# One 512-column matmul for both operand parts in the last products of the 256-token stages

## What is computed

```
h = h + 0.5 * (silu(n @ w_gate) * (n @ w_up)) @ w_down      # feed-forward, 2816 wide
h = h + concat(y_ret, y_diff) @ w_out                       # mixer of the first block
h = h + (b_gate * conv) @ w_out                             # short convolution
h = h + o @ w_out                                           # dilated attention
```

## Time and profile before

| | us |
|---|---|
| median of 3 runs | 2353.56 (2352.23 to 2355.72) |
| the profiled execution | 2352.63 |
| its span (first to last instruction) | 2350.8 |
| PE busy | 2292.0 (97%) |
| PE weight load busy | 2218.0 (94%) |
| DVE busy | 1527.3 (65%) |
| ACT busy | 1161.2 (49%) |

### The profile page before, as it was taken

The page is one execution under the profiler, slowest core; times in us unless marked ns, Lnnn a source line. Parts: engine busy times, 40 slices in busy tenths (PEclk is TensorE's granted clock), DMA queues, the critical chain, the costliest instruction groups (busy, mean ns, idle before and its releaser), DMA issues.

```text
span 2350.8 us, 42875 instructions
## 1 busy us (share of the span) xinstructions
PE 2292.0 (97%) x18162; PEld 2218.0 (94%) x18162; DVE 1527.3 (65%) x2626; ACT 1161.2 (49%) x1826; POOL 35.3 (2%) x47
## 2 busy tenths in 40 slices
PE   7999999999999998999999999999999899999999
PEld 7999878999999987999999999999999798988999
DVE  6665966665665675766676587656665666665763
ACT  5444455444544454644554445445444556564542
POOL 0000000100000000000000000000000000000000
PEclk9999999999999999999999999999999999999999
DMA  8545423865555432554565465555555444452653
GB/s 279 177 155 172 144 90 113 260 212 176 177 171 170 158 126 73 186 190 163 174 214 173 157 216 196 182 170 191 195 173 158 137 139 138 141 167 81 215 188 99
DMA packets 423454, 393.65 MB, mean 167 GB/s; under 512 B 14015, under 2 KB 419647, under 8 KB 423264
## 3 DMA queue, kind: packets, MB, share of 16 engines
q1 hardware_dynamic: 412240, 375.56, 49.5%
q0 software_dynamic: 11024, 15.36, 2.1%
HBM read 389.66 MB, written 7.41 MB: 169 GB/s over the span
## 4 chain that ended last, share of the span: by engine, by line
PE 91%; DVE 6%; ACT 2%; issue 1%; DMA 1%; SPq 0%; DVEq 0%; ACTq 0%
PE ps L1236 28%; PE ps L1237 28%; PE ps L1238 28%; DVE t L805 2%; PE ps L1480 1%; PE ps L1500 1%; PE ps L1455 1%; PE ps L1491 0%; PE ps L1482 0%; PE ps L1502 0%; PE ps L1347 0%; PE ps L1348 0%; PE ps L1340 0%; DVE t L833 0%; DMA t<-ffn_w_gate 0%
## 5 line engine op out<-in xcount | busy, mean ns | idle before, releaser
L1236 PE MATMUL ps<-t 128*128 128x256 f32 (+1 forms) x5696 | 1638.6, 288 | 21.8 <-DVE t L805 17.1
L1237 PE MATMUL ps<-t 128*128 128x256 f32 (+1 forms) x5696 | 1626.0, 285 | 0.0
L1238 PE MATMUL ps<-t 128*128 128x256 f32 (+1 forms) x5696 | 1621.0, 285 | 0.0
L1236 PEld LDWEIGHTS ps<-t 128*128 128x128 f32 x5696 | 1080.4, 190 | 39.1 <-issue 29.7
L1237 PEld LDWEIGHTS ps<-t 128*128 128x128 f32 x5696 | 1078.7, 189 | 5.2 <-issue 4.4
L1238 PEld LDWEIGHTS ps<-t 128*128 128x128 f32 x5696 | 1079.3, 189 | 0.0
L805 DVE TENSOR_TENSOR t<-t 128x1024 fp32r<-128x1024 f32 (+1 forms) x728 | 862.1, 1196 | 184.7 <-ACT t L550 183.1
L550 ACT ACTIVATE t<-t 128x1024 fp32r<-128x1024 f32 (+1 forms) x728 | 737.7, 1029 | 315.3 <-PE ps L1238 303.8
L625 ACT ACTIVATE t<-t 128x256 fp32r<-128x256 f32 (+1 forms) x176 | 74.5, 423 | 307.2 <-DVE t L931 307.2
L928 DVE TENSOR_TENSOR t<-ps,t 128x256 f32<-128x256 f32 (+1 forms) x176 | 75.6, 430 | 128.3 <-PE ps L1238 128.3
L921 DVE TENSOR_TENSOR t<-ps,t 128x256 f32<-128x256 f32 (+1 forms) x176 | 75.7, 430 | 116.0 <-PE ps L1238 114.9
(11 more groups left out here) (155 smaller groups left out, 978.2 us busy)
## 6 DMA issues: line engine op xcount, KB each, us to landing
t<-ffn_w_in SPq DMA_DIRECT2D x88, 1024.0 KB, 5.2
t<-ffn_w_gate SPq DMA_DIRECT2D x43, 1024.0 KB, 5.2
t<-ffn_w_up SPq DMA_DIRECT2D x43, 1024.0 KB, 5.4
t<-attn_w_qkv SPq DMA_DIRECT2D x72, 512.0 KB, 3.6
t<-ffn_w_down SPq DMA_DIRECT2D x32, 1024.0 KB, 5.3
t<-ffn_w_out SPq DMA_DIRECT2D x32, 1024.0 KB, 5.3
t<-w_in SPq DMA_DIRECT2D x28, 1024.0 KB, 4.9
t<-ffn_w_down SPq DMA_DIRECT2D x16, 768.0 KB, 4.8
```

The source lines that it names most:

```text
L1236: pe.matmul(o, hi, xhi, start=i == 0, stop=False)
L1237: pe.matmul(o, hi, xlo, start=False, stop=False)
L1238: ins = pe.matmul(o, lo, xhi, start=False, stop=i == r.nk - 1)
```

## The change

In the last products of the stages with 256 tokens (feed-forward stages 5, 6, 8, 9 and 11, mixer stage 4, convolution stage 7, dilated stage 10) a group has two matmuls in place of three. The first multiplies the high weight part with both operand parts, 512 columns in one instruction, over the whole bank: columns 0 to 255 get hi.xhi, columns 256 to 511 hi.xlo. The second adds lo.xhi to columns 0 to 255. DVE adds each half of the bank to `h` with an instruction of its own; the second waits for the first, and it, not the first, counts up `evac`. All other products stay as they were.

```diff
-                        dve.scalar_tensor_tensor(h[:, m, c0:T], ps[:, r.banks[j], 0:T - c0], scale, h[:, m, c0:T],
+                        ins = dve.scalar_tensor_tensor(h[:, m, c0:T], ps[:, r.banks[j], 0:T - c0], scale, h[:, m, c0:T],
+                                                       ALU.mult, ALU.add)
+                        if c0 == 0:
+                            ins.then_inc(S["evac"], 1)
+                        else:
+                            ins.then_inc(S["dve"], 1)
+                            own.up()
+                    for j in range(r.n if c0 else 0):
+                        m = r.first - first + j
+                        w.wait_ge(S["dve"], own.n - r.n + 1 + j)
+                        dve.scalar_tensor_tensor(h[:, m, c0:T], ps[:, r.banks[j], SEQ:2 * SEQ], scale, h[:, m, c0:T],
                                                  ALU.mult, ALU.add).then_inc(S["evac"], 1)
...
-                        pe.matmul(o, hi, xhi, start=i == 0, stop=False)
-                        pe.matmul(o, hi, xlo, start=False, stop=False)
+                        if both is None:
+                            pe.matmul(o, hi, xhi, start=i == 0, stop=False)
+                            pe.matmul(o, hi, xlo, start=False, stop=False)
+                        else:
+
+                            pe.matmul(ps[:, r.banks[j], :], hi, both(k), start=i == 0, stop=False)
                         ins = pe.matmul(o, lo, xhi, start=False, stop=i == r.nk - 1)
...
-                        matmuls(r, range(FCH), lambda k: (a[:, k, 0, 0:N], a[:, k, 1, 0:N]), ready)
+                        matmuls(r, range(FCH), lambda k: (a[:, k, 0, 0:N], a[:, k, 1, 0:N]), ready,
+                                both=(lambda k: a[:, k, :, 0:N]) if N == SEQ else None)
...
+                            (lambda k: y[:, k, :, cq:T]) if NQ == SEQ else None)
...
+                            both=lambda k: c_yy[:, k, :, :])
...
+                            both=lambda k: d_y[:, k, :, :])
```

More of the change, by code:

```diff
@@ L1218, in _, with matmuls @@
             w = Waits(pe)
-            def matmuls(r, order, operand, ready, hook=None):
+            def matmuls(r, order, operand, ready, hook=None, both=None):
                 N = T - r.c0
@@ L1426, in mixer @@
                         w.wait_ge(S["hn"], at(l, "r", 3))
-                    matmuls(r, OUT_ORDER, lambda k: (y[:, k, 0, cq:T], y[:, k, 1, cq:T]), ready, hook if m == 0 else None)
+                    matmuls(r, OUT_ORDER, lambda k: (y[:, k, 0, cq:T], y[:, k, 1, cq:T]), ready, hook if m == 0 else None,
+                            (lambda k: y[:, k, :, cq:T]) if NQ == SEQ else None)
             def conv(s):
@@ L1439, in conv @@
                 for r in runs[21:]:
-                    matmuls(r, range(KC), lambda k: (c_yy[:, k, 0, :], c_yy[:, k, 1, :]), ready)
+                    matmuls(r, range(KC), lambda k: (c_yy[:, k, 0, :], c_yy[:, k, 1, :]), ready,
+                            both=lambda k: c_yy[:, k, :, :])
             def dilated(s):
@@ L1517, in dilated @@
                         w.wait_ge(S["hyl"], NH)
-                    matmuls(r, range(KC), lambda k: (d_y[:, k, 0, :], d_y[:, k, 1, :]), ready)
+                    matmuls(r, range(KC), lambda k: (d_y[:, k, 0, :], d_y[:, k, 1, :]), ready,
+                            both=lambda k: d_y[:, k, :, :])
             w.wait_ge(S["square"], 16)
```

## The result

| | before | after |
|---|---|---|
| median of 19 runs, us | 2353.31 (2351.8 to 2355.72) | 2358.56 (2354.33 to 2361.51) |
| ratio | | 1.0022, 95% interval 1.0015 to 1.0029 |
| span of the profiled execution, us | 2350.8 | 2356.9 |

The kernel became slower by 5.2 us, 0.22%. I had forecast 0.5 us less, had given 0.60 to no measurable change and 0.15 to slower. The time lies inside the range, at its upper end, and just inside the case that had 0.15; the likeliest case was wrong.

What follows compares the result with a forecast made beforehand. PE's matmuls were taken to bound the kernel. -10.4 (fixed part) + 2.3 + 3.9 (DVE) + 0.7 (last evictions) = -3.5 us; 3.0 us of low clock makes -0.5, so 2353.1 us, range 2345 to 2359.5.

Steps and rivals of the forecast that it cites:

- The DVE part: Second evictions delay the low weight part PE waits for: 2.3 us more in stage 4, 3.9 in stages 7 and 10.
- PE's head start: In stages 7 and 10 PE is earlier by 24 groups x 11.8 ns = 0.28 us, taken off DVE's delay.
- the low part of the fourth tile: Low weight part from DVE for the next stage's first run; PE starts on it 2.3 us later in stage 4.
- the last evictions: At the kernel's end four evictions in place of two, 0.33 us apart: 0.7 us more before the last transfer.
- The term that failed is the fixed part of the wide matmul: Time a 512-column matmul holds PE besides its columns: 11.8 ns, saving 10.4 us over 880 feed-forward groups.
- My bounds: Limits of the 512-column matmul's fixed part from plain float32 rows: 3.3 ns saves 17.9 us, 20 ns saves 3.3 us.
- The slower rival: Fixed part 20 ns, a group saves 3.7 ns, and the waits come: +7.0 us, 2360.6 us; chance 0.13.
- The clock's sum: PE's new waits bring two low-clock stretches, behind stage 4 and one of stages 7 and 10: 3.0 us more.
- A wide matmul without a fixed part: Rival: the 512-column matmul has nearly no fixed part (3.3 ns), -8.4 us, 2345.2 us; chance 0.15.
- delays that don't reach PE: Rival: slack in the ACT and DVE chain hides DVE's delays, -9.7 us, 2343.9 us; chance 0.07.
- no low clock: Rival: PE's new waits bring no stretch at 1.2 GHz, -3.5 us, 2350.1 us; chance 0.10.
- The 2.5 ns of the Trainium skill: Warm gap of columns / 2.4 plus 2.5 ns; 880 groups would save 2.2 us, and the kernel would be +8.1 us.

Runs made afterwards that it cites:

- e3: Split eviction alone in all eight stages, with three 256-column matmuls a group as in the kernel before; ratio 1.0047 to the kernel before, median 2365.89 us.
- e2: Wide matmul and split eviction only in stages 4, 7 and 10, feed-forward stages as in the kernel before; ratio 1.0037 to the kernel before, median 2364.15 us.
- e8: The whole change, with the feed-forward operand of the 256-token stages stored as one unbroken row of 512; one run, wide matmul 230.6 ns.
- e5: The whole change, but DVE makes low weight parts of m0 to m5 right behind their evictions in stages 4, 7, 10; ratio 0.9962 to the kernel before, median 2344.63 us.

## Why the prediction was wrong, point by point

**The DVE part was right.** Forecast for the ends of the stages: +2.3 us in stage 4 and, before PE's head start, about +2.25 in stages 7 and 10, at the low part of the fourth tile. Measured: +2.28, +2.24 and +2.24. e3 shows that the split alone does it. Of the last evictions 0.7 us was forecast; from the first of them to the end of the span it is 3.70 us against 3.03, 0.67.

**The term that failed is the fixed part of the wide matmul.** "I take 11.8, because two widths of the same type gave it and it didn't move with the width." The widths were 256 and 272, the one wanted was 512. It is 17.4, a group saves 6.6 ns and five feed-forward stages 5.9 us, not 10.4. This is 4.5 of the 5.7 us between the forecast change (-0.5) and the measured one (+5.2).

My bounds (3.3 and 20 ns) held the value, but by luck. The 20 was read as the mean of six distances, and these aren't equal:

```profile
1900.75 0.48 PE L1480 MATMUL ps<-t 64*128 64x256 f32 x1
1901.07 0.38 PE L1480 MATMUL ps<-t 64*128 64x256 f32 x1
1901.29 0.38 PE L1480 MATMUL ps<-t 64*128 64x256 f32 x1
```

The first is 0.32 us and the other five 0.216, so a 256-column float32 matmul has a fixed part of 2.7 ns, and 20 is no fixed part of any. The 512-column one, at 428 ns, has 1.3. No row of the kernel before shows anything like 17.4: the rows read rightly leave 1.3 to 11.9 ns. The slower rival had this very mechanism, at 3.7 ns saved; the truth lay between it and the forecast, and 6.6 ns is under the 7.8 from which it decides without any low clock. I had given it 0.13.

**The clock's sum was near, its parts were not.** Two short stretches of 1.5 us were taken, 3.0 us together. In stage 4 a stretch came in every trace with the split eviction there (the changed kernel, e2, e3, e8), each time with PEclk at 0.50 for 6.8 us (957.1 to 963.9 in the changed kernel), and it cost 2.5 us. Behind the waits of stages 7 and 10, of 2.1 to 2.5 us, it came in three of the eight places that these four traces have (stage 7 of e2 and e8, stage 10 of e3), for 3.4 us each, and where e2 and the changed kernel differ by it in stage 7, it is 1.5 us. That it hangs on the wait, e5 shows: no wait, no low stretch. The length of the standstill alone doesn't decide: 2.45 us in stage 7 of the changed kernel brought none, 2.09 in stage 10 of e3 brought one. The clock's share at these places is 2.5 us in the profiled pair and 4.0 in e2, e3 and e8, on either side of the 3.0 of the sum: the cause was right, and the sizes of its parts were not.

**The sum with the measured terms.** -5.9 + 2.3 + 2 x 2.15 + 0.7 = +1.4 us, and 2.5 for the clock in stage 4 = +3.9. The medians have +5.25. The remaining 1.3 us have two candidates that the traces show: a low stretch behind stage 7 or 10, and the low stretches near the start of stage 10, which cost up to 2.4 us more from one trace to another with the same last product there. The wider scatter of the changed kernel (7.2 us, against 3.9 of before) fits the first. With one trace of each kernel it isn't shown which it is, so it stays open.

**The rivals.** A wide matmul without a fixed part, delays that don't reach PE, and no low clock are all refuted. The 2.5 ns of the Trainium skill, from the section named above, would have given the right sign (+8.1 us in the prediction), but for another reason: the fixed part is far above 2.5 ns at both widths.

## What to carry to other kernels

A merged instruction saves what one instruction costs beside its data only if the larger one costs no more of that; read it at the size it will have, or take the bound that hurts. Where a change lengthens an engine's work ahead of something that the bound engine takes with 0.2 us to spare, all of the length but those 0.2 us lands on the path, and an idle PE can bring a stretch of half clock on top. Look then for another order of the same work: here it turned +0.2% into -0.4%.

## What the runs showed of the hardware that I had not expected

- The fixed part of an fp32r matmul depends on its width and its neighbours: 11.8 ns each for a row of matmuls of 256 columns, 17.4 at 512 in front of a 256, and for 384 / 256 in one segment only 19.4 for both together.
- A second segment in the moving operand (the one that streams its columns through) costs 5 ns at 2x128 columns. The groups with 2x192 and 2x256 cost 10 ns more and 2 less than those with one segment, but there the operand of the narrow matmul behind lies another way in memory too; with 2x256 that one takes 118 ns with the gap (the changed kernel) and 120 without it (e8).
- A standstill of PE of 2.78 us in stage 4 (955.55 to 958.32) brought half clock in four traces of four, one of 2.1 to 2.5 us in stages 7 and 10 in three of eight; the low stretches lasted 6.8 us in stage 4 and 3.4 us in stages 7 and 10.
